# The operand tiles and the split weights of an f32r matmul stream, placed 64 bytes past a multiple of 128

## The chip, the cores and the metric

The kernel runs on one core of a Trainium2 chip. The metric is the time of one execution on the device in microseconds (us); the median of the three runs before the change is 1978.26 us (1977.85 to 1979.46).

## The reference

Two transformer-like layers on a sequence of 256 tokens, width 2048, all in float32. The first layer:

```python
h = _rmsnorm(x, pre_norm_g)
proj = h @ w_in                       # 2048 -> 1088 + 7 * 2048 columns, split into ten parts
q  = _rmsnorm(q_a)  @ w_q_b           # 512 -> 16 heads * 192
kv = _rmsnorm(c_kv) @ w_kv_b          # 512 -> 16 heads * 256
attn   = causal_attention(q, kv) * silu(z_mla);           y_mla  = attn @ w_o_mla
y_conv = (b_gate * conv3(c_gate * c_in) * silu(z_conv)) @ w_o_conv
merged = sigmoid(g_mla) * y_mla + sigmoid(g_conv) * y_conv
x = x + _rmsnorm(merged @ w_out, post_norm_g)
```

The second layer puts 16 learned rows (`meta_tokens_2`) ahead of the 256 tokens, projects 272 rows with `w_in_2` (2048 to 12368 columns), runs a top-64 attention with an indexer on 8 heads and a gated linear recurrence on 8 heads, and joins both branches:

```python
p = einsum('btnc,ncd->btnd', stack([y_a, y_b], 2), w_branch)   # two times 1024 -> 2048
merged = sum(sigmoid(gates) * p, axis=2)
h = h + merged @ w_out_2
```

What bears on this case is that nearly all of the arithmetic is matrix products of some 84 million weights (335 MB read from HBM) with 256 or 272 rows.

## The kernel before

**Units.** Activations are kept transposed: features on the 128 partitions, the 256 tokens along the free dimension. A weight matrix is worked through in units of at most 1024 elements for each partition: for most stages two k-tiles (128 input features each) of 512 output columns, that is four tiles of 128 columns; for the stage `qi` one k-tile of 1024 columns, eight tiles. `phases()` lists the stages in the order in which they run. Their matmuls are issued by `tile` in `tensor_engine`, through the helper `mm` (L1267, so that nearly every matmul carries this line).

**Split products.** Float32 precision comes from a high and a low part of both operands. For each unit, a DMA on SyncE fills one of four slots of `w_raw`; ScalarE rounds it to f32r into one of three slots of `w_hi` (`split_hi`, L1592), VectorE subtracts to get `w_lo` (`split_lo`, L1895). Activations are split in the same way into the tiles of `hb_hi`, `hb_lo` and `ob_hi`, `ob_lo`, one tile for each of 16 k-tiles. For each k-tile of each output tile, TensorE runs three matmuls: moving x_hi against the stationary w_hi, then x_lo against w_hi, then x_hi against w_lo. Each has its own load of the 128x128 stationary tile (PEld in the profile), which runs while the matmul ahead of it streams.

**Who reads which operand.** `Memory.operand` says it. `hb` is the moving operand of the stages with operand h, mg, ya and yb (the later k-tiles 8 to 15 for yb). `ob` is that of the latent projections (lat_q, lat_kv), oconv (oc), omla (zm), all second-layer projections (h2: 256 tokens from column 16 on; h2_all: all 272 columns) and the last product wout2 (mg2). In wout2 and in half of the stage kv the roles are turned: the activation tile is stationary and the weights move, in wout2 512 columns at a time.

**Places in memory.** `Memory.__init__` allocates the tensors one after another in each partition. `w_raw` begins at byte 16512, which is 129 times 128. Its 4 slots have 4096 bytes each, as have the 3 slots each of `w_hi` and `w_lo`. The four operand tensors have 16 tiles of 272 columns, 1088 bytes each, of which the 256-column stages use 1024 bytes: columns 0 to 255 in `hb` and for lat, oc and zm in `ob`, columns 16 to 271 in `ob` for h2. All seven tensors therefore begin 128 bytes past a multiple of 256.

**What sets the order.** `plan_work` fixes one order of steps for all engines ahead of time, with rings for PSUM banks, scratch tiles and slots; side work (attention, norms, recurrence) is taken in by `pump()` between units. The engines then run their own queues in that order and meet through semaphores.

Of the kernel before, what the change touches and what calls it, by code (L numbers as in the profile page):

```python
# [8 lines left out]
F32 = mybir.dt.float32  # L9
F32R = mybir.dt.float32r  # L10
I32 = mybir.dt.int32
U8 = mybir.dt.uint8
ALU = mybir.AluOpType
ACT = mybir.ActivationFunctionType
AX = mybir.AxisListType.X

P = 128
D = 2048
KT = D // P
S = 256  # L20
NMETA = 16
T = S + NMETA
# [95 lines left out]
class Stream:  # L118
# [3 lines left out]
    def __init__(self, eng, own):  # L122
        self.eng, self.own, self.count, self.seen = eng, own, 0, {}
# [67 lines left out]
class Phase:  # L191


    def __init__(self, name, weight, groups, ktiles, operand, n, period=1, pairs=False, hold=False):
        self.name, self.weight, self.groups, self.ktiles = name, weight, groups, ktiles
        self.operand, self.n, self.period, self.pairs, self.hold = operand, n, period, pairs, hold
# [827 lines left out]
PARTS1 = ((0, P), (P, 3 * P))  # L1024
HD = DN + RD
W2 = 2 * S
MAGIC = 1.5 * 2.0 ** 23
N_LVL = len(LEVELS) * P // 2
L0 = CONSTS["late"][0]
# [5 lines left out]
class Memory:  # L1035


    def __init__(self, nc, ctx, a):
        def sb(name, shape, dt=F32):
            return ctx.enter_context(nc.sbuf_tensor(name, shape, dt))  # L1040

        self.raw = sb("w_raw", [P, N_RAW, UNIT])
        self.whi = sb("w_hi", [P, N_SPLIT, UNIT], F32R)
        self.wlo = sb("w_lo", [P, N_SPLIT, UNIT], F32R)
        self.hb_hi, self.hb_lo = (sb(n, [P, KT, T], F32R)[:, :, 0:S] for n in ("hb_hi", "hb_lo"))
        self.ob_hi, self.ob_lo = sb("ob_hi", [P, KT, T], F32R), sb("ob_lo", [P, KT, T], F32R)
        self.arena = sb("arena", [P, 72 * 256])
        self.con = sb("con", [P, CONSTS["resident"][1]])
        self.cols = sb("cols", [P, P])
        self.rope1 = sb("rope1", [P, 2, S])  # L1050
        self.fac = sb("factor", [P, 3, T])
        self.small = sb("small", [P, 256])
        self.scratch = [sb(f"scratch{i}", [P, T])[:, :] for i in range(5)]
        self.heads = [sb(f"head_factor{i}", [P, T])[:, :] for i in range(3)]
        self.acc_a, self.acc_b = sb("acc_a", [P, S])[:, :], sb("acc_b", [P, S])[:, :]
        psum = [ctx.enter_context(nc.psum_tensor(f"bank{i}", [P, 512], F32))[:, :] for i in range(8)]
        self.proj, self.side = psum[:5], psum[5:]
        self.stats = [sb(f"stats{i}", [P, 8])[:, :] for i in range(6)]
        self.prob = [sb(f"prob{i}", [P, 416])[:, :] for i in range(2)]
        self.prob_t = [sb(f"probT{i}", [P, 384])[:, :] for i in range(2)]  # L1060
        self.small2, small3 = sb("small2", [P, 64]), sb("small3", [P, 2 * HI])
        self.q_factor = sb("q_factor", [P, 2 * HA])
        self.best = sb("best", [P, 16])

        r = self.region
        self.Q1, self.QR, self.K1 = r(0, 16, H1, S), r(16, 8, H1 // 2, S), r(24, 16, H1, S)
        self.V1, self.G1 = r(40, 16, 2, D), r(56, 16, KT, S)
        self.LAT = self.V1[:, 0, :].rearrange("p (k n) -> p k n", k=8)
        self.OUT1, self.GM, self.XR = r(40, 16, KT, S), self.K1, r(24, 16, KT, S)
        self.x_in, self.x_meta, self.xT = r(0, 16, 2, D), r(16, 8, D), self.G1  # L1070
        self.rows_in, self.pos_i = r(24, 1, P), r(25, 1, S)[0:1, :].bitcast(I32)
        self.u_t, self.gate_t = r(56, 4, 4, S), r(60, 4, 4, S)
        self.kr1 = r(68, 1, S)
        self.KR2, self.KI2 = r(64, 2, 2, S), r(48, 2.25, 2, T)
        self.pos_f, self.metaT = self.small[0:1, 0:S], self.small[:, :]
        self.metaf = self.metaT.rearrange("p (k n) -> p k n", k=KT)
        s2 = self.small2
        self.lb, self.oml, self.lbx, self.mx = s2[:, 0:8], s2[:, 8:16], s2[:, 16:32], s2[:, 32:40]
        self.acc_m, self.rkv_col, self.q_gain = s2[:, 40:56], s2[:, 56:58], s2[:, 58:59]
        self.wiT = small3[:, :]  # L1080
        self.R, self.RR, self.RQ = self.fac[:, 0, 0:S], self.fac[:, 1, 0:S], self.fac[:, 2, 0:S]
        self.F2 = self.fac[:, 1, :]
        self.F2M = self.F2[:, NMETA:T]

        self.QI, self.KI = r(0, 8, 8, S), r(8, 2, T)
        self.KA, self.QA, self.VA = r(9.25, 4.25, KVA, T), r(13.5, 8, HA, S), r(21.5, 6, 3, 512)
        self.FB, self.IB, self.QB = r(27.5, 8.5, HB, T), r(36, 12, 3, 1024), r(48, 8, HB, S)
        self.GA, self.GB = r(56, 16, KT, S), r(29, 16, KT, S)
        self.late = r(58, 6, CONSTS["late"][1] - L0)
        self.bias2, self.score2 = r(65, 2, 416), r(67, 2, 416)  # L1090
        self.lvl, self.lvl_in = self.small[:, 0:N_LVL // 4].bitcast(U8), r(69, 2, N_LVL)
        self.prob_m = [self.rope1[:, i, :] for i in range(2)]
        self.Cb, self.Rb, self.kL, self.qL = r(0, 2, W2), r(2, 2, W2), r(4, 2, W2), r(6, 2, W2)
        self.A, self.kK, self.kd, self.St, self.kM = r(8, 2, W2), r(10, 2, W2), r(12, 1, S), r(21.5, 2, W2), r(23.5, 4, 1024)
        self.xT2, self.OT = r(29, 16, KT, S), r(0, 16, 2, D)

        self.x_dram = nc.dram_tensor("x_kept", [P, KT * S], F32, kind="Internal").ap()
        self.x1_dram = nc.dram_tensor("x1_kept", [P, KT * S], F32, kind="Internal").ap()
        self.weights = {n: a[n] for n in ("w_in", "w_q_b", "w_kv_b", "w_o_conv", "w_o_mla", "w_out")}
        self.weights |= {"w_in_2": a["w_in_2"][0], "w_branch_a": a["w_branch_2"][0, 0],  # L1100
                         "w_branch_b": a["w_branch_2"][0, 1], "w_out_2": a["w_out_2"][0]}
# [20 lines left out]
    def operand(self, name, k):  # L1122

        if name in ("h", "mg", "ya"):
            return self.hb_hi[:, k, :], self.hb_lo[:, k, :]
        if name == "yb":
            return self.hb_hi[:, k + 8, :], self.hb_lo[:, k + 8, :]
        if name == "h2":
            return self.ob_hi[:, k, NMETA:T], self.ob_lo[:, k, NMETA:T]
        if name == "h2_all":  # L1130
            return self.ob_hi[:, k, :], self.ob_lo[:, k, :]
        k += 4 * (name == "lat_kv")
        return self.ob_hi[:, k, 0:S], self.ob_lo[:, k, 0:S]

    def out_of(self, u, m, bank):

# [439 lines left out]
def scalar_engine(nc, m, a, plan, S_):  # L1576

    sc, done, act = Stream(nc.scalar, S_("act_own")), plan.done, nc.scalar.activation
# [57 lines left out]
    def latent_split(s):  # L1636
        which, t = s.args
        k = 4 * (which == "kv") + t
        sc.wait_ge(*s.of["x"])
        sc.wait_ge(*done["cols"])  # L1640
        act(m.ob_hi[:, k, 0:S], m.LAT[:, k, :], ACT.Copy, scale=m.col(which + "a", t)).then_inc(S_("op_hi"), 1)

    def v(s):
        g, blk = s.args
# [40 lines left out]
    def conv_split(s):  # L1685
        j, t = s.args
        k = 4 * j + t
        sc.wait_ge(*s.of["y"])
        sc.wait_ge(*done["lat_used"])
        act(m.ob_hi[:, k, 0:S], m.u_t[:, t, :], ACT.Copy).then_inc(S_("op_hi"), 1)  # L1690

    def gate(s):
        name, k = s.args
# [159 lines left out]
    def x1_turn(s):  # L1853
# [6 lines left out]

    does = dict(first_loads=first_loads, split_hi=split_hi, constants=constants, x_tile=x_tile, x_keep=x_keep, sine=sine,
                bounds_exp=bounds_exp, meta_turn=meta_turn, latent=latent, latent_split=latent_split, v=v,
                scores1=scores1, turn1=turn1, mix1=mix1, cgate=cgate, zconv=zconv, conv_split=conv_split, gate=gate,
                z_sig=z_sig, z_split=z_split, merge_split=merge_split, out1=out1, meta_scale=meta_scale,
# [17 lines left out]
def vector_engine(nc, m, plan, S_):  # L1882
# [3 lines left out]
    tt, ts, stt = v.tensor_tensor, v.tensor_scalar, v.scalar_tensor_tensor  # L1886
# [59 lines left out]
    def turns(s):  # L1946
# [5 lines left out]
        ve.wait_ge(*t)  # L1952
        ve.step(ts(k_, k_, MAGIC, MAGIC, ALU.add, ALU.subtract))

# [52 lines left out]
    def latent_split(s):  # L2007
        which, t = s.args
        k = 4 * (which == "kv") + t
        ve.wait_ge(*s["op_hi"])  # L2010
        stt(m.ob_lo[:, k, 0:S], m.LAT[:, k, :], m.col(which + "a", t), m.ob_hi[:, k, 0:S].bitcast(F32),
            ALU.mult, ALU.subtract).then_inc(S_("op_lo"), 1)

    def kr(s):
# [83 lines left out]
    def conv_split(s):  # L2098
        j, t = s.args
        k = 4 * j + t  # L2100
        ve.wait_ge(*s["op_hi"])
        tt(m.ob_lo[:, k, 0:S], m.u_t[:, t, :], m.ob_hi[:, k, 0:S].bitcast(F32), ALU.subtract).then_inc(S_("op_lo"), 1)

    def gate(s):
        name, k = s.args
# [471 lines left out]
```

## Time and profile before

| | us |
|---|---|
| median of 3 runs | 1978.26 |
| the profiled execution | 1978.3 |
| its span, first to last instruction | 1977.0 |
| PE busy | 1952.0 (15786 matmuls) |
| PEld busy | 1920.3 |
| DVE busy | 1176.7 |
| ACT busy | 879.2 |
| POOL busy | 317.0 |
| DMA, mean rate | 174 GB/s |

Busy times are sums of the time in which an engine had an instruction under way. Matmuls are pipelined: one that the profile gives as 0.28 us long is followed by the next 0.12 us later, so for a stream of them the distance between starts is the measure, not the length. The distance is read either from two rows of the timeline and the number of matmuls between them, or from a window laid from the first start of a stage to the first start of the next.

### The profile page before, as it was taken

The numbers are of one execution on the slowest core, as the hardware profiler recorded it, in microseconds if no ns is written. First come the engines' busy times: TensorE is split into PE (matmuls) and PEld (weight loads), VectorE is DVE, ScalarE is ACT, GpSimd is POOL, SyncE is SP. The second block draws the span as 40 slices with busy tenths as digits, with TensorE's granted clock in tenths as the row PEclk, the third lists the DMA queues.
The fourth block names the chain that finished last, engine by engine and source line by source line (L and its number), as shares of the span: only waits on it lengthen the run. The fifth ranks groups of instructions, "written<-read, shape, count | busy, mean of one in ns | idle before, by whom it ended". The sixth has DMA issues, their size and how long they took to land.

```text
span 1977.0 us, 37092 instructions
## 1 busy us (share of the span) xinstructions
PE 1952.0 (99%) x15786; PEld 1920.3 (97%) x15786; DVE 1176.7 (60%) x1707; ACT 879.2 (44%) x1264; POOL 317.0 (16%) x320
## 2 busy tenths in 40 slices
PE   7999999999999999999999999999999999999999
PEld 7999999999999999999999999999999999999987
DVE  6765665655554445654554574676457687564644
ACT  5444454444444434544444543445443333444443
POOL 3110010202010001300121253040011132110200
PEclk9999999999999999999999999999999999999999
DMA  7565445555555555555565564443555444565564
GB/s 248 155 192 177 153 148 159 161 180 182 184 185 187 183 189 183 182 183 189 183 226 185 165 213 139 139 140 117 158 177 155 139 131 138 180 193 184 183 232 159
DMA packets 175647, 343.79 MB, mean 174 GB/s; under 512 B 10478, under 2 KB 19050, under 8 KB 174954
## 3 DMA queue, kind: packets, MB, share of 16 engines
q1 hardware_dynamic: 174106, 337.16, 53.7%
q10 hardware_dynamic: 1376, 4.26, 0.6%
q8 instruction: 124, 2.03, 0.4%
q14 instruction: 41, 0.34, 0.0%
HBM read 335.09 MB, written 6.29 MB: 173 GB/s over the span
## 4 chain that ended last, share of the span: by engine, by line
PE 92%; DVE 2%; issue 1%; ACT 1%; POOL 0%; POOLq 0%; ACTq 0%; DVEq 0%
PE bank L1267 91%; DVE w_lo L1895 1%; ACT w_hi L1592 0%; DVE arena L2166 0%; DVE hb_lo L2127 0%; DVE ob_lo L2171 0%; DVE arena L2160 0%; DVE scratch L1997 0%; POOL scratch L2487 0%; PE bank L1474 0%; PE bank L1563 0%; PE bank L1414 0%; PE bank L1413 0%; PE bank L1412 0%; PE bank L1564 0%
## 5 line engine op out<-in xcount | busy, mean ns | idle before, releaser
L1895 DVE TENSOR_TENSOR w_lo<-w_raw,w_hi 128x1024 fp32r<-128x1024 f32 (+2 forms) x644 | 786.0, 1225 | 502.0 <-ACT w_hi L1592 500.0
L1592 ACT ACTIVATE w_hi<-w_raw 128x1024 fp32r<-128x1024 f32 (+2 forms) x644 | 662.4, 1031 | 910.8 <-PE bank L1267 905.8
L1267 PE MATMUL bank<-hb_hi,w_hi 128*128 128x256 f32 x2448 | 697.9, 285 | 3.2 <-DVE w_lo L1895 3.2
L1267 PE MATMUL bank<-hb_hi,w_lo 128*128 128x256 f32 x2448 | 690.0, 282 | 0.0
L1267 PE MATMUL bank<-hb_lo,w_hi 128*128 128x256 f32 x2448 | 688.2, 281 | 0.0
L1267 PE MATMUL bank<-ob_hi,w_hi 128*128 128x256 f32 (+1 forms) x2224 | 645.7, 290 | 5.1 <-DVE ob_lo L2171 2.6
L1267 PE MATMUL bank<-ob_hi,w_lo 128*128 128x256 f32 (+1 forms) x2224 | 627.4, 282 | 0.0
L1267 PE MATMUL bank<-ob_lo,w_hi 128*128 128x256 f32 (+1 forms) x2224 | 626.3, 282 | 0.0
L1267 PEld LDWEIGHTS bank<-hb_hi,w_hi 128*128 128x128 f32 x2448 | 464.7, 190 | 5.3 <-DVE w_lo L1895 3.9
L1267 PEld LDWEIGHTS bank<-hb_hi,w_lo 128*128 128x128 f32 x2448 | 462.5, 189 | 0.0
L1267 PEld LDWEIGHTS bank<-hb_lo,w_hi 128*128 128x128 f32 x2448 | 461.7, 189 | 0.4
L1267 PEld LDWEIGHTS bank<-ob_hi,w_hi 128*128 128x128 f32 x2224 | 420.4, 189 | 8.2 <-DVE w_lo L1895 3.6
L1267 PEld LDWEIGHTS bank<-ob_lo,w_hi 128*128 128x128 f32 x2224 | 420.2, 189 | 1.5
L1267 PEld LDWEIGHTS bank<-ob_hi,w_lo 128*128 128x128 f32 x2224 | 419.5, 189 | 0.0
L1267 PE MATMUL bank<-arena 128*128 128x64 f32 (+4 forms) x618 | 101.6, 302 | 2.5 <-ACT arena L1812 1.5
L1267 PEld LDWEIGHTS bank<-arena 128*128 128x128 f32 x618 | 80.8, 191 | 4.8 <-ACT arena L1812 2.3
L2497 POOL TENSOR_TENSOR arena<-scratch,arena 128x256 f32<-128x256 f32 x32 | 38.4, 1225 | 272.8 <-DVE scratch L1997 272.8
L1997 DVE TENSOR_TENSOR scratch<-bank,factor 128x256 f32<-128x256 f32 (+1 forms) x132 | 52.7, 420 | 39.4 <-PE bank L1267 38.6
L1267 PE MATMUL bank<-w_hi,ob_hi 128*128 128x512 f32 (+1 forms) x192 | 69.0, 359 | 0.0
L1267 PE MATMUL bank<-w_lo,ob_hi 128*128 128x512 f32 (+1 forms) x192 | 68.5, 357 | 0.0
L1267 PE MATMUL bank<-w_hi,ob_lo 128*128 128x512 f32 (+1 forms) x192 | 68.4, 356 | 0.0
L2470 POOL TENSOR_TENSOR arena<-arena,factor 128x256 f32<-128x256 f32 x16 | 19.2, 1226 | 272.8 <-DVE arena L1997 272.8
(237 smaller groups left out, 1209.8 us busy)
## 6 DMA issues: line engine op xcount, KB each, us to landing
w_raw<-in_w_in SPq DMA_DIRECT2D x436, 512.0 KB, 3.5
w_raw<-in_w_out SPq DMA_DIRECT2D x64, 512.0 KB, 4.2
w_raw<-in_w_o_conv SPq DMA_DIRECT2D x32, 512.0 KB, 3.7
w_raw<-in_w_o_mla SPq DMA_DIRECT2D x32, 512.0 KB, 3.7
w_raw<-in_w_branch SPq DMA_DIRECT2D x32, 512.0 KB, 3.5
w_raw<-in_w_kv_b SPq DMA_DIRECT2D x16, 512.0 KB, 3.7
w_raw<-in_w_q_b SPq DMA_DIRECT2D x16, 384.0 KB, 3.3
arena<-x_kept SPq DMA_DIRECT2D x2, 2048.0 KB, 8.9
```

The source lines that it names most:

```text
L1267: return nc.tensor.matmul(dst, lhsT, rhs, start=start, stop=stop, skip_group_check=True)
L1592: act(dst, src, ACT.Copy).then_inc(S_("w_hi"), 1)
L1895: tt(low, src, high.bitcast(F32), ALU.subtract).then_inc(S_("w_lo"), 1)
L1997: tt(dst, m.proj[s.of["pb"]][:, 0:dst.shape[1]], factor, ALU.mult).then_inc(S_("evac"), 1)
L2470: tt(m.u_t[:, t, :], m.u_t[:, t, :], m.R, ALU.mult).then_inc(S_("conv_b"), 1)
L2497: tt(y, m.scratch[s.of["scratch"].slot][:, 0:S], y, ALU.add).then_inc(S_("merged"), 1)
```

## The change

The diff adds an unused tensor of 16 floats (64 bytes) ahead of `w_hi`, so that the split weights and all that follows move by 64 bytes. `hb_hi` and `hb_lo` become the two halves of one tensor whose tiles follow each other every 1024 bytes, with 16 floats of padding behind it. The tiles of `ob_hi` and `ob_lo` become 288 columns (1152 bytes) apart, and the stages that use 256 of them all take columns 16 to 271; lat, oc and zm used columns 0 to 255 before. No instruction is added or removed, and none changes its size. `w_raw` stays where it is; `arena` and the tensors behind it move by 128 bytes as a whole.

```diff
@@ -1024,6 +1024,7 @@
 W2 = 2 * S
+ODD = 16
 MAGIC = 1.5 * 2.0 ** 23
@@ -1040,10 +1041,12 @@
         self.raw = sb("w_raw", [P, N_RAW, UNIT])
+        sb("odd", [P, ODD])
         self.whi = sb("w_hi", [P, N_SPLIT, UNIT], F32R)
         self.wlo = sb("w_lo", [P, N_SPLIT, UNIT], F32R)
-        self.hb_hi, self.hb_lo = (sb(n, [P, KT, T], F32R)[:, :, 0:S] for n in ("hb_hi", "hb_lo"))
-        self.ob_hi, self.ob_lo = sb("ob_hi", [P, KT, T], F32R), sb("ob_lo", [P, KT, T], F32R)
+        hb = sb("hb", [P, 2 * KT * S + ODD], F32R)[:, 0:2 * KT * S].rearrange("p (k n) -> p k n", k=2 * KT)
+        self.hb_hi, self.hb_lo = hb[:, 0:KT, :], hb[:, KT:2 * KT, :]
+        self.ob_hi, self.ob_lo = (sb(n, [P, KT, T + ODD], F32R)[:, :, 0:T] for n in ("ob_hi", "ob_lo"))
         self.arena = sb("arena", [P, 72 * 256])
@@ -1130,7 +1133,7 @@
         k += 4 * (name == "lat_kv")
-        return self.ob_hi[:, k, 0:S], self.ob_lo[:, k, 0:S]
+        return self.ob_hi[:, k, NMETA:T], self.ob_lo[:, k, NMETA:T]
@@ -1638,7 +1641,7 @@
-        act(m.ob_hi[:, k, 0:S], m.LAT[:, k, :], ACT.Copy, scale=m.col(which + "a", t)).then_inc(S_("op_hi"), 1)
+        act(m.ob_hi[:, k, NMETA:T], m.LAT[:, k, :], ACT.Copy, scale=m.col(which + "a", t)).then_inc(S_("op_hi"), 1)
...
```

The three places left out (L1690, L2011, L2102) make the same replacement of `0:S` by `NMETA:T` where ScalarE and VectorE write these tiles.

## Rows read from the trace of the kernel before

**Rows 1.** The page: busy time by engine, granted clock, and the chain that ended last.
```profile
PE 1952.0 (99%) x15786; PEld 1920.3 (97%) x15786; DVE 1176.7 (60%) x1707; ACT 879.2 (44%) x1264; POOL 317.0 (16%) x320
...
PEclk9999999999999999999999999999999999999999
...
PE 92%; DVE 2%; issue 1%; ACT 1%; POOL 0%; POOLq 0%; ACTq 0%; DVEq 0%
```
**Rows 2.** Groups of PE by form: count | busy us, mean ns | idle before, releaser.
```profile
L1267 PE MATMUL bank<-hb_hi,w_hi 128*128 128x256 f32 x2448 | 697.9, 285 | 3.2 <-DVE w_lo L1895 3.2
...
L1267 PE MATMUL bank<-ob_hi,w_hi 128*128 128x256 f32 x1824 | 524.2, 287 | 5.1 <-DVE ob_lo L2171 2.6 <-DVE w_lo L1895 2.4
...
L1267 PE MATMUL bank<-ob_hi,w_hi 128*128 128x272 f32 x400 | 121.5, 304 | 0.0
...
L1267 PE MATMUL bank<-w_hi,ob_hi 128*128 128x512 f32 x128 | 51.0, 398 | 0.0
```
**Rows 3.** Windows of oconv, gmla, part of gb, bb: length, PE busy (x), clock.
```profile
653.45:744.66 91.21, 91.21 (x771) 1.00 0.56 185
836.25:927.64 91.39, 91.39 (x770) 1.00 0.58 185
1757.02:1824.72 67.70, 67.70 (x579) 1.00 0.63 194
1836.00:1881.39 45.39, 45.39 (x386) 1.00 0.55 183
```
**Rows 4.** Timeline of stage qi: first matmul of nine units; and one later matmul.
```profile
1122.66 0.28 PE L1267 MATMUL bank<-ob_hi,w_hi 128*128 128x256 f32 x1
...
1125.51 0.28 PE L1267 MATMUL bank<-ob_hi,w_hi 128*128 128x256 f32 x1
...
1128.23 0.28 PE L1267 MATMUL bank<-ob_hi,w_hi 128*128 128x256 f32 x1
...
1131.09 0.28 PE L1267 MATMUL bank<-ob_hi,w_hi 128*128 128x256 f32 x1
...
1133.92 0.28 PE L1267 MATMUL bank<-ob_hi,w_hi 128*128 128x256 f32 x1
...
1136.76 0.28 PE L1267 MATMUL bank<-ob_hi,w_hi 128*128 128x256 f32 x1
...
1139.59 0.28 PE L1267 MATMUL bank<-ob_hi,w_hi 128*128 128x256 f32 x1
...
1140.54 0.28 PE L1267 MATMUL bank<-ob_hi,w_lo 128*128 128x256 f32 x1
...
1142.46 0.28 PE L1267 MATMUL bank<-ob_hi,w_hi 128*128 128x256 f32 x1
...
1145.29 0.28 PE L1267 MATMUL bank<-ob_hi,w_hi 128*128 128x256 f32 x1
```
**Rows 5.** Timeline of wout2: first two matmuls of two units, one after the other.
```profile
1929.39 0.39 PE L1267 MATMUL bank<-w_hi,ob_hi 128*128 128x512 f32 x1
1929.62 0.40 PE L1267 MATMUL bank<-w_hi,ob_lo 128*128 128x512 f32 x1
...
1932.17 0.40 PE L1267 MATMUL bank<-w_hi,ob_hi 128*128 128x512 f32 x1
1932.41 0.39 PE L1267 MATMUL bank<-w_hi,ob_lo 128*128 128x512 f32 x1
```
**Rows 6.** Timeline of oconv: three matmuls of k-tile 0 against the second weight tile.
```profile
654.16 0.29 PE L1267 MATMUL bank<-ob_hi,w_hi 128*128 128x256 f32 x1
...
654.53 0.28 PE L1267 MATMUL bank<-ob_hi,w_hi 128*128 128x256 f32 x1
```

More of the change, by code:

```diff
@@ L1689, in conv_split @@
         sc.wait_ge(*done["lat_used"])
-        act(m.ob_hi[:, k, 0:S], m.u_t[:, t, :], ACT.Copy).then_inc(S_("op_hi"), 1)
+        act(m.ob_hi[:, k, NMETA:T], m.u_t[:, t, :], ACT.Copy).then_inc(S_("op_hi"), 1)
     def gate(s):
@@ L2010, in latent_split @@
         ve.wait_ge(*s["op_hi"])
-        stt(m.ob_lo[:, k, 0:S], m.LAT[:, k, :], m.col(which + "a", t), m.ob_hi[:, k, 0:S].bitcast(F32),
+        stt(m.ob_lo[:, k, NMETA:T], m.LAT[:, k, :], m.col(which + "a", t), m.ob_hi[:, k, NMETA:T].bitcast(F32),
             ALU.mult, ALU.subtract).then_inc(S_("op_lo"), 1)
@@ L2101, in conv_split @@
         ve.wait_ge(*s["op_hi"])
-        tt(m.ob_lo[:, k, 0:S], m.u_t[:, t, :], m.ob_hi[:, k, 0:S].bitcast(F32), ALU.subtract).then_inc(S_("op_lo"), 1)
+        tt(m.ob_lo[:, k, NMETA:T], m.u_t[:, t, :], m.ob_hi[:, k, NMETA:T].bitcast(F32), ALU.subtract).then_inc(S_("op_lo"), 1)
     def gate(s):
```

## The prediction

> **What bounds the kernel.** I read the page first: TensorE is busy for 99% of the span, at full granted clock in all 40 slices, and the chain that ended last is PE for 92% [rows 1]. VectorE at 60%, ScalarE at 44% and the DMA have room. The groups by form say what TensorE does: 2448 triples of 256-column matmuls that move `hb`, 1824 that move `ob`, 400 of 272 columns, 128 that move 512 weight columns, with 3.2 and 5.1 us of waiting ahead of the two largest groups [rows 2]. So the time is a count of matmuls times the distance between their starts, and nothing that other engines do matters unless it makes TensorE wait.
>
> The windows give that distance. In oconv 768 matmuls take 91.21 us, 118.8 ns each; gmla, which moves `hb`, 91.39 us, 119.0 ns; 576 of gb 67.70 us, 117.5 ns; the 384 of bb 45.39 us, 118.2 ns [rows 3]. (The counts in these rows have two or three more, which began before the window.) 256 columns at 2.4 GHz are 106.7 ns, so some 11 ns of each step are something else, and the step differs between stages whose instructions are the same. Nothing waits in these windows: busy equals length.
>
> **Where the step depends on place.** Stage qi is a natural experiment, because there one activation tile moves for a whole unit of 24 matmuls. What counts for me is the distance of the moving tile from the stationary tile, modulo 256 bytes. The weights all lie 128 past a multiple of 256, and tile k of h2 lies 128 + 64 + 1088k, so the distance is 64(k+1) modulo 256. The first rows of nine units [rows 4] give, divided by 24:
> - k = 2, distance 192: 2.72 us, 113.3 ns. k = 6, the same distance: 2.83 us, 117.9 ns.
> - k = 4 and 8, distance 64: 2.83 us each, 117.9 ns.
> - k = 1 and 5, distance 128: 2.85 and 2.84 us, 118.8 and 118.3 ns.
> - k = 3 and 7, distance 0: 2.86 and 2.87 us, 119.2 and 119.6 ns; once settled, the last 16 steps of k = 7 take 1142.46 - 1140.54 = 1.92 us, 120.0 ns.
>
> Two things follow: place is worth up to 6.7 ns a step, and a place can hold more than one rhythm (113.3 and 117.9 at 192).
>
> Is it the distance, or the moving tile's own place? In wout2 the weights move and their place modulo 256 never changes; the stationary activation tile does. Two units that follow each other begin with a step of 0.23 us and one of 0.24 us [rows 5], and in the timeline this pattern alternates with the pairs of stationary tiles (k = 0, 1 against k = 2, 3). The place of the stationary tile therefore counts too, which is what two reads that get in each other's way would do. I take the distance as what decides.
>
> **The change, part by part.**
> - `hb`: before, its tiles stood at distances 0, 64, 128, 192 in turn. After, the weights lie 192 past a multiple of 256, and so does every tile of `hb`, which is 1024 bytes long: distance 0, for all 2448 triples. Both were moved by the same 64 bytes. The bounds are 119.2 ns, the unit k = 3 [rows 4], and the worst triple at distance 0, the one in oconv, 654.53 - 654.16 = 0.37 us or 123 ns a step [rows 6]; I take the settled 120.0, since here nothing leaves distance 0. Of the 7344 matmuls, 6576 (h, mg) stood at 118.8 by oconv, which walks through the same four distances: +1.2 x 6576 = +7.9 us. The 768 of ya and yb stood at bb's 118.2: +1.8 x 768 = +1.4 us.
> - `ob`, 256 columns: a tile is 1152 bytes, so used from column 16 the tiles lie 64 and 192 past a multiple of 256 in turn: distances 128 and 0. Mean of 118.5 and 120.0: 119.3 ns (bounds 118.3 and 120.0). The 2016 matmuls of oc, zm, lat_q and lat_kv stood at 118.8: +0.5 x 2016 = +1.0 us. The 3456 of h2 stood at gb's 117.5: +1.8 x 3456 = +6.2 us. This is half the cost though these tiles hardly move: h2 already lay 64 past in half its tiles, and it loses the 192 that gives 113.3.
> - `ob`, 272 columns (h2_all, 1200 matmuls): now 0 and 128, distances 64 and 192, the good ones. At 256 columns the mean of these (117.9, and 113.3 or 117.9) is 116.8, that of all four about 117.9: -1.1 x 1200 = -1.3 us.
> - wout2 and the turned half of kv (576 matmuls): distances 128 and 0 instead of four. Rows 5 show steps of 0.23 and 0.24 us at different places; at 1 ns either way this is ±0.6 us, taken as 0.
> - Writes of the split tiles by ScalarE and VectorE keep their sizes; w_raw's DMA is unchanged. If they grew by a few per cent, the 40% of VectorE's span that is free would hide it. The 64 bytes of `odd` cost no instruction. `arena`, `con` and the rest move together, so side matmuls keep their distances: 0.
>
> Sum: 7.9 + 1.4 + 1.0 + 6.2 - 1.3 = +15.2 us. The profiled execution took 1978.3 us (span 1977.0), as the median does (1978.26). Where TensorE waits for a split, a slower step is absorbed; with 3.2 + 5.1 us of such idle [rows 2] I take off 0.5. That gives 1993.0 us, 0.75% slower. The likeliest case's own range is 1984 (119.2 for `hb`, 118.3 for `ob`) to 2001.
>
> The Trainium skill speaks against any of this: "TensorE: Matmul & The Clock Gate", Part 2, step 1, says that TensorE has two independent read ports, so that loading the next tile's weights takes no bandwidth from the running matmul, and its formula for the back-to-back gap, N/2.4 + 2.5, would be 109 ns at 256 columns wherever the operands lie. The trace disagrees, with 113.3 to 120.0 ns in one stage [rows 4].
>
> **The rivals.**
> - *Only the moving tile's own place counts* (0.19). Then rows 4 read by absolute place: 192 past a multiple of 256 (k = 4, 8) is 117.9, 64 past (k = 2, 6) 113.3 or 117.9, mean 115.6; 0 and 128 past are the slow ones, and the change moves all 256-column tiles off them. `hb` all at 117.9: -0.9 x 6576 - 0.3 x 768 = -6.1 us; `ob` at the mean of 117.9 and 115.6, 116.8: -2.0 x 2016 - 0.7 x 3456 = -6.5 us; h2_all goes to the slow places, +1.3. Sum -11.3: 1967 us, faster. For it: every odd multiple of 64 is below every even one in rows 4. Against it: wout2, where the stationary place shows. It wins if that influence is small for 256 columns.
> - *Distance 0, held throughout, settles in a quicker rhythm* (0.08). Distance 192 has two, 4.6 ns apart. At 118 ns `hb` would save 0.8 x 6576 + 0.2 x 768 = 5.4 us and `ob` cost some 4: 1976 us, within or a little past no change. Against it: units k = 3 and 7 come from different neighbours and both go to 120.
> - *It does nothing* (0.06): the step follows the order of instructions and not places, and the patterns of rows 4 are an accident of it. 1978.3 us. The reads being independent, as the page above has it, would give this.
> - *A worse rhythm at distance 0* (0.03): 123 ns as in rows 6 for all of `hb`: +4.5 x 7344 = +33 us, 2018 us with `ob`. Against it: such triples stand only right after a change of distance.
>
> **How the numbers follow.** The likeliest case has 0.64. A measurement of this kernel tells 0.2%, about 4 us, from no change. Slower by more than that: 0.62 of the likeliest, the worse rhythm's 0.03 and 0.01 of the quicker rhythm's case, 0.66. Within: 0.02 + 0.06 + 0.04 = 0.12. Faster: 0.19 + 0.03 = 0.22. The range runs from 1966 to 2001: it leaves out half of the first rival, the worse rhythm and the tail of the likeliest.
>
> **What would show it.** If I am right, gmla's window is 768 x 120.0 = 92.2 us instead of 91.39 and bb's 46.1 instead of 45.39; units of qi take 2.84 to 2.88 us and none 2.72; the 272-column groups have lower means. If the moving place alone counts, gmla's window is 90.5 us. If `hb` stages keep steps of different lengths although their distance never changes, the picture of two reads that meet modulo 256 bytes is wrong as such. Idle time of TensorE should stay as it is in every case.

## The result, and the profile after

The changed kernel takes 1987.82 us, the median of four runs (1987.09 to 1988.31), against 1978.18 before: a ratio of 1.0047 [1.003, 1.0065]. It is slower, by 9.6 us where the forecast had 14.7. The profiled execution has a span of 1985.8 us, 8.8 more than before.

The page after, busy time by engine, granted clock and the chain that ended last:

```profile
PE 1961.1 (99%) x15786; PEld 1930.5 (97%) x15786; DVE 1177.1 (59%) x1707; ACT 880.0 (44%) x1264; POOL 316.7 (16%) x320
...
PEclk9999999999999999999999999999999999999999
...
PE 92%; DVE 2%; ACT 1%; issue 1%; POOL 0%; POOLq 0%; ACTq 0%
```

Against [rows 1], PE is busy for 9.1 us more with the same 15786 instructions and the same granted clock (0.998 on the mean of both spans); the load of the stationary tiles (PEld) for 10.2 us more, and the other engines stand within 1 us. So the time came from inside the stream of matmuls, and not from a wait.

The groups of PE by form after (count | busy us, mean ns | idle before, releaser):

```profile
L1270 PE MATMUL bank<-hb,w_hi 128*128 128x256 f32 x4896 | 890.1, 284 | 3.0 <-DVE w_lo L1898 2.9
...
L1270 PE MATMUL bank<-ob_hi,w_hi 128*128 128x256 f32 x1824 | 522.1, 286 | 4.9 <-DVE ob_lo L2174 2.6 <-DVE w_lo L1898 2.3
...
L1270 PE MATMUL bank<-ob_hi,w_hi 128*128 128x272 f32 x400 | 121.1, 303 | 0.0
```

`hb` is one tensor now, so its first two products share a name and a row (4896 = 2 x 2448). Idle time ahead of the two largest groups is 3.0 and 4.9 us, where [rows 2] had 3.2 and 5.1. The mean durations hardly tell anything (286 for 287 ns on `ob_hi` though its stages changed in both directions): a pipelined matmul's length is not its step.

The steps are in the windows of oconv, gmla, omla, gb and bb, each from its first start to the next stage's first start (length, PE busy (x), clock, ...):

```profile
657.11:747.57 90.46, 90.46 (x770) 1.00 0.59 187
839.85:932.07 92.22, 92.22 (x771) 1.00 0.62 183
932.07:1023.37 91.30, 91.30 (x770) 1.00 0.57 185
1752.73:1844.20 91.47, 91.47 (x771) 1.00 0.62 184
1844.20:1890.28 46.08, 46.08 (x387) 1.00 0.57 181
```

bb has 384 matmuls in 46.08 us: 120.0 ns. gmla's 92.22 us are 120.1 ns for 768, and 759 of its steps in the trace are 120 ns to the nanosecond. Both are what the prediction wrote down, 46.1 and 92.2. But oconv went down, from 91.21 [rows 3] to 90.46 us, which is 117.8 ns a step, while omla, with the same instructions on the same operand addresses, takes 91.30 us, 118.9 ns.

The timeline of stage qi after, the first matmul of six units, k = 1 to 6:

```profile
1127.97 0.28 PE L1270 MATMUL bank<-ob_hi,w_hi 128*128 128x256 f32 x1
...
1130.84 0.28 PE L1270 MATMUL bank<-ob_hi,w_hi 128*128 128x256 f32 x1
...
1133.69 0.28 PE L1270 MATMUL bank<-ob_hi,w_hi 128*128 128x256 f32 x1
...
1136.56 0.28 PE L1270 MATMUL bank<-ob_hi,w_hi 128*128 128x256 f32 x1
...
1139.42 0.28 PE L1270 MATMUL bank<-ob_hi,w_hi 128*128 128x256 f32 x1
...
1142.29 0.28 PE L1270 MATMUL bank<-ob_hi,w_hi 128*128 128x256 f32 x1
```

The first five units take 2.87, 2.85, 2.87, 2.86, 2.87 us, and the next three, in the trace, between 2.85 and 2.88. Odd k stand at distance 0 now and even k at 128. The quick unit of 2.72 us in [rows 4] is gone, as predicted. Step by step (starts to the nanosecond), distance 0 settles at 120, 120, 120, ..., and distance 128 repeats 119, 115, 118, 122, 120: the same five steps that units at distance 128 showed before the change, when they lay at other places. These distances differ by whole multiples of 256 bytes from unit to unit (the tiles lie 1152 bytes apart), and all eight units at distance 0 settle at 120 ns; so it is the distance modulo 256 that counts.

One thing is not as foreseen. In gconv, whose moving tiles all stand at distance 0, 558 of the 768 steps are not 120 ns: from the 79th step on the trace shows 124, 118, 117, 121, 120, over and over, and a part of zmla does the same. The mean of these five is 120.0 too, so no time comes of it (gconv takes 92.26 us, gmla 92.22), but one distance does not mean one step.

### The profile page after: what moved, and what is told of

Its sections match the earlier page's. It is cut to its first block, busy times and chain, and to the rows that moved or that the text cites. A ratio compares the mean times of both kernels' runs of the same rounds, so it can differ in the third digit from the quotient of the medians.

```text
span 1985.8 us, 37092 instructions
## 1 busy us (share of the span) xinstructions
PE 1961.1 (99%) x15786; PEld 1930.5 (97%) x15786; DVE 1177.1 (59%) x1707; ACT 880.0 (44%) x1264; POOL 316.7 (16%) x320
## 4 chain that ended last, share of the span: by engine, by line
PE 92%; DVE 2%; ACT 1%; issue 1%; POOL 0%; POOLq 0%; ACTq 0%
PE bank L1270 91%; DVE w_lo L1898 1%; DVE arena L2169 1%; ACT w_hi L1595 0%; DVE ob_lo L2174 0%; DVE arena L2163 0%; POOL scratch L2490 0%; PE bank L1477 0%; PE bank L1415 0%; PE bank L1567 0%; PE bank L1417 0%; PE bank L1566 0%; PE bank L1416 0%; PE bank L1479 0%; ACT ob_hi L1750 0%
## 5 line engine op out<-in xcount | busy, mean ns | idle before, releaser
L1270 PE MATMUL bank<-hb,w_hi 128*128 128x256 f32 x4896 | 890.1, 284 | 3.0 <-DVE w_lo L1898 2.9
L1270 PEld LDWEIGHTS bank<-hb,w_hi 128*128 128x128 f32 x4896 | 764.1, 192 | 4.9 <-DVE w_lo L1898 3.6
L1270 PE MATMUL bank<-hb,w_lo 128*128 128x256 f32 x2448 | 693.1, 283 | 0.0
L1270 PEld LDWEIGHTS bank<-hb,w_lo 128*128 128x128 f32 x2448 | 469.1, 192 | 0.0
L2490 POOL TENSOR_TENSOR scratch<-scratch,head_factor 128x256 f32<-128x256 f32 x16 | 12.6, 786 | 242.6 <-ACT head_factor L1708 242.6
L2000 DVE TENSOR_TENSOR arena<-bank,factor 128x256 f32<-128x256 f32 (+1 forms) x86 | 34.6, 421 | 24.5 <-PE bank L1270 24.3
```

Source lines behind the costliest of these rows:

```text
L1270: return nc.tensor.matmul(dst, lhsT, rhs, start=start, stop=stop, skip_group_check=True)
L2000: tt(dst, m.proj[s.of["pb"]][:, 0:dst.shape[1]], factor, ALU.mult).then_inc(S_("evac"), 1)
L2490: tt(z, z, ring[s.of["head"].slot][:, 0:S], ALU.mult).then_inc(S_("silu"), 1)
```

## The experiments

Three kernels (`e1_sweep`, `e4_rhythms`, `e8_pairs`) are streams of matmuls alone and leave out the whole computation but for rounding one block of `w_in` to f32r; the others compute all of it. In a stream, "step" is the distance between starts, from the trace.

**1. A stream at sixteen distances.** The body of the loop is the kernel's triple, on a pool of f32r data:

```python
w = w0 // 4 + 128 * (m % 4)
x = (w0 + ds[m % len(ds)]) // 4
wh, wl = pool[:, w:w + 128], pool[:, WL + w:WL + w + 128]
xh, xl = pool[:, XH + x:XH + x + n], pool[:, XL + x:XL + x + n]
nc.tensor.matmul(dst, wh, xh, start=m % 2 == 0, stop=False, skip_group_check=True)
nc.tensor.matmul(dst, wh, xl, start=False, stop=False, skip_group_check=True)
inst = nc.tensor.matmul(dst, wl, xh, start=False, stop=m % 2 == 1, skip_group_check=True)
```

Here `w0` is the place of the weights and `ds` the distance, or the distances in turn, in bytes.

> Leaves the whole computation out but for a stream of f32r matmuls on one place of memory; only the distance between starts is of use. Blocks of 96 matmuls of 256 columns in the kernel's order (x_hi by w_hi, x_lo by w_hi, x_hi by w_lo, four weight tiles in turn), the moving tile d = 0, 16, ... 240 bytes past a multiple of 1024 while the weights stay at one; then blocks with weights and tile both moved by 64 and by 32 bytes, short blocks that change d in every order, blocks of 512 and of 128 columns, and blocks whose tile alternates. Theory 1 (the distance of the moving from the stationary tile modulo 256 decides): d = 0 settles at 120.0 ns, 64 at 117.8, 128 at 118.6, 192 at 113.3 or 117.8, and the blocks moved by 64 or 32 as a whole repeat these to 0.3 ns. Theory 2 (each tile's own place counts): the blocks moved by 64 differ from the unmoved ones of the same distance by 1 ns or more. Theory 3 (the rhythm is set by the order of instructions, not by place): all blocks of 256 columns lie within 1 ns. At 128 columns the weight load should be the bound, with the same step of about 113 ns as the quickest rhythm at 256; at 512 I expect 225 to 235 ns.

Windows of `e1_sweep`: 96 matmuls of 256 columns each at distance 64, 112, 128, 192; then 48 each at distances 0, 64, 128 and 192 with weights and moving tile both 64 bytes on; then 48 of 512 columns at distance 0 and 192; then 96 of 128 columns at distance 0 and 192:

```profile
70.20:81.51 11.31, 11.31 (x99) 1.00 0.01 1
...
104.55:115.43 10.88, 10.88 (x99) 1.00 0.01 2
115.43:126.81 11.38, 11.38 (x99) 1.00 0.01 1
160.92:171.81 10.89, 10.89 (x99) 1.00 0.01 2
205.86:211.60 5.74, 5.74 (x50) 1.00 0.00 0
211.60:217.26 5.66, 5.66 (x51) 1.00 0.01 3
217.26:222.96 5.70, 5.70 (x51) 1.00 0.00 0
222.96:228.43 5.47, 5.47 (x50) 1.00 0.00 0
...
299.17:310.07 10.90, 10.90 (x50) 1.00 0.00 0
332.23:343.43 11.20, 11.20 (x49) 1.00 0.01 1
343.43:354.10 10.67, 10.67 (x97) 1.00 0.00 0
...
375.54:386.26 10.72, 10.72 (x98) 1.00 0.01 2
```

The mean of the last 24 steps of each block at 256 columns, worked out from the starts (the last of them is the step into the next block):

| distance | 0 | 16 | 32 | 48 | 64 | 80 | 96 | 112 |
|---|---|---|---|---|---|---|---|---|
| ns | 120.0 | 118.7 | 116.7 | 118.3 | 117.8 | 120.0 | 120.0 | 113.3 |

| distance | 128 | 144 | 160 | 176 | 192 | 208 | 224 | 240 |
|---|---|---|---|---|---|---|---|---|
| ns | 118.7 | 118.5 | 117.3 | 119.3 | 113.3 | 119.2 | 118.3 | 117.4 |

There is no other work here, next to no DMA (a share of 0.01) and no side matmul. What is left to differ is the place, and what ran before, which the short blocks below show. With both operands moved together by 64 bytes the steps settle at 120.0, 117.8, 118.8 and 113.3 again, and by 32 bytes the same: the distance decides, and not where either operand lies. Two more readings. At 512 columns the order is turned round: 226.7 ns at distance 0 (10.90 us / 48 is 227), 228.9 at 64, 232.3 at 128, 233.3 at 192. At 128 columns all four distances settle at a mean of 111.7 ns, though 128 columns are only 53 ns at 2.4 GHz: there something that does not depend on distance sets the step. The load of the stationary tile, which has the same size in all cases, is my guess; no run tests it.

Short blocks of 24 in the same run enter one distance from another. Distance 192 entered from 0 or 128 goes to 113.3, entered from 64 it keeps the 117.8 that 64 had; 128 settles either in the five steps (118.8 on the mean) or in 118, 120, 122 (120.0). Which rhythm a distance takes depends on what ran before it.

**2. The tiles moved, the weights not.** The unused tensor goes behind the weights, so that `hb` stands at distance 64 and the 256-column tiles of `ob` at 192 and 64 in turn:

```diff
         self.raw = sb("w_raw", [P, N_RAW, UNIT])
-        sb("odd", [P, ODD])
         self.whi = sb("w_hi", [P, N_SPLIT, UNIT], F32R)
         self.wlo = sb("w_lo", [P, N_SPLIT, UNIT], F32R)
+        sb("odd", [P, ODD])
```

> The changed kernel with the 64 bytes of odd behind w_lo instead of ahead of w_hi: the operand tiles lie exactly where the change puts them, the weights where they were. Distances: 64 for all of hb, 192 and 64 in turn for ob at 256 columns, 128 and 0 for h2_all. Theory 1 (distance decides): hb at 117.8, 1.0 below before, ob between 115.6 and 117.8: 10 to 14 us faster than before, 1964 to 1968 us, ratio 0.993 to 0.995. Theory 2 (the tiles' own place decides): as the changed kernel, 1988 us, ratio 1.005. Theory 3 (neither): 1978 us.

It takes 1965.89 us, a ratio of 0.9935 [0.9922, 0.9949]. The windows of oconv, gmla, gb and bb:

```profile
646.18:735.78 89.60, 89.60 (x770) 1.00 0.60 189
826.56:917.30 90.74, 90.72 (x771) 1.00 0.63 186
1733.51:1823.50 89.99, 89.88 (x771) 1.00 0.63 187
1823.49:1868.72 45.23, 45.23 (x386) 1.00 0.58 186
```

bb's 45.23 us are 117.8 ns, the step of distance 64 in the stream. Every moving tile lies exactly where it lies in the changed kernel, since the 64 bytes stand ahead of `hb` in both; only the weights differ, and 22 us lie between the two kernels. With the 64 bytes behind the weights instead of ahead of them, the change would have made the kernel faster. oconv settles at 116.7 ns. At distance 64, cin0 ran at 113.3 and cgate0 at 115.0 before the stages went to 117.8, and zmla ran at 116.7, so 64 has more than one rhythm as well.

**3. `hb` alone at distance 0**, on multiples of 128 bytes, with nothing moved by 64. This is the `hb` term of the sum by itself, at other places than the change has it:

```diff
-        self.hb_hi, self.hb_lo = (sb(n, [P, KT, T], F32R)[:, :, 0:S] for n in ("hb_hi", "hb_lo"))
+        hb = sb("hb", [P, 2 * KT * S], F32R)[:, :].rearrange("p (k n) -> p k n", k=2 * KT)
+        self.hb_hi, self.hb_lo = hb[:, 0:KT, :], hb[:, KT:2 * KT, :]
```

> The kernel before with one edit: the tiles of hb lie every 1024 bytes, so all at a multiple of 128 and at distance 0 from the weights, which are not moved; ob as before. Nothing lies 64 past a multiple of 128 in hb. Theory 1 (distance decides): the hb stages run at 120.0 ns a matmul as in the changed kernel, +9 us, ratio 1.0045 to 1.005. Theory 2 (it is lying 64 past a multiple of 128 that made the changed kernel slower): not slower than before, 1976 to 1979 us.

1986.28 us, 1.0041 [1.0028, 1.0054]. Windows of oconv, gmla, gb, bb:

```profile
658.57:749.78 91.21, 91.21 (x771) 1.00 0.59 185
841.99:934.24 92.25, 92.25 (x770) 1.00 0.62 183
1753.51:1844.10 90.59, 90.55 (x771) 1.00 0.63 186
1844.10:1890.17 46.07, 46.07 (x386) 1.00 0.57 183
```

The stages of `hb` are those of the changed kernel (92.22 and 46.08 there), those of `ob` are those of before ([rows 3]; oconv 91.21). So 7.8 us (1986.28 - 1978.44, the median of the kernel before that was taken beside it) are the price of `hb` at distance 0, and all the rest of the change is worth about 1.8 us (9.6 - 7.8).

**4. How firm each rhythm is.** A stream in which one of five different sets of float32 side matmuls runs ahead of each block of 36, at 23 distances:

```python
for c in ((128, 128), (256,), (1, 1, 1), (128, 128, 128), (64, 64, 64, 64))[j]:
    nc.tensor.matmul(dst[:, 0:c], raw[:, 0:128], raw[:, 512:512 + c], start=True, stop=True, skip_group_check=True)
...
```

Twelve triples as in experiment 1 follow each set.

> As e1_sweep leaves the whole computation out; a stream of f32r matmuls of 256 columns with fixed weights' place. For each distance 0, 16, ... 240 and for 4, 8, 12, 104, 108, 116, 120 bytes, five blocks of 36 matmuls, each entered after a different few float32 matmuls of 128, 256, 1 or 64 columns, as side work in the kernel does. Theory A (each distance has a small set of steady rhythms and the disturbance picks one): all five blocks of a distance end in one of at most two or three means; 0 always ends at 120.0, 192 and 64 at 113.3 or 117.8. Theory B (the rhythm belongs to the distance alone): the five blocks of a distance end alike, and those of e1_sweep's place are repeated: 112 and 192 at 113.3, 32 at 116.7, 64 at 117.8.

The last 23 steps of two blocks at distance 112 and two at 192 (after the third and the fourth set):

```profile
207.88:210.49 2.61, 2.61 (x26) 1.00 0.00 0
212.68:215.29 2.61, 2.61 (x26) 1.00 0.00 0
...
329.67:332.38 2.71, 2.71 (x25) 1.00 0.00 0
334.55:337.16 2.61, 2.61 (x25) 1.00 0.00 0
```

2.61 us / 23 is 113.5 ns, 2.71 / 23 is 117.8. Of the five blocks at 192 one settles at 113.3 and four at 117.8; at 112 all five settle at 113.3; at 0 four stand at 120.0 and one comes to it within its last 12 steps (119.1); at 64 three stand at 117.8 and two at 113.3. Off the multiples of 16 there are worse places: 123.3 ns at 4, 116.7 or 126.7 at 8, up to 130 at 104. So a distance gives a short list of rhythms, and what ran before picks one of them. Distance 0 has only one mean, and it is a slow one; the kernel's gconv showed that two patterns of steps (120 throughout, and the five) share it.

**5. `hb` alone at distance 192**, every 1024 bytes:

```diff
-        self.hb_hi, self.hb_lo = (sb(n, [P, KT, T], F32R)[:, :, 0:S] for n in ("hb_hi", "hb_lo"))
+        hb = sb("hb", [P, 2 * KT * S + 64], F32R)[:, 48:48 + 2 * KT * S].rearrange("p (k n) -> p k n", k=2 * KT)
+        self.hb_hi, self.hb_lo = hb[:, 0:KT, :], hb[:, KT:2 * KT, :]
```

> The kernel before with the tiles of hb every 1024 bytes and all at distance 192 from the weights, which stay; ob as before. Distance theory: the hb stages run at 113.3 ns where the quick rhythm holds and at 117.8 where it does not. All quick: 6576 x 5.4 + 768 x 4.9 = 39 us faster, 1939 us; all slow: 6576 x 0.95 + 768 x 0.4 = 6.5 us faster, 1972 us. I expect stretches of both, as after side work in the first stage of e2_tiles_only (113.4 in cin0, then 117.8): 1960 to 1972 us, ratio 0.991 to 0.997. If it were only the 64 bytes past a multiple of 128 that help, all stages would go at 117.8: 1972 us.

1944.33 us (1942.78 to 1944.83), 0.9825 [0.9812, 0.9838]. Windows of oconv, gmla, gb, bb, and the first row of what PE waits for (us in total, times, longest):

```profile
633.70:724.47 90.77, 90.77 (x770) 1.00 0.59 187
813.98:901.66 87.68, 87.64 (x771) 1.00 0.66 192
1713.44:1804.03 90.59, 90.55 (x770) 1.00 0.63 186
1804.03:1847.56 43.53, 43.53 (x386) 1.00 0.60 191
```

```profile
PE bank L1268 <- DVE w_lo L1896: 7.4, 8, 3.0
```

bb's 43.53 us are 113.4 ns. That misses what was expected, 1960 to 1972 us with stretches of both rhythms: the quick one held in nearly all stages of `hb`. At 5.4 ns a step less than before (118.75 - 113.33), 7344 matmuls could give 40 us; 34 came. About 2 of the missing 6 us are new waiting: TensorE waits for `w_lo` in 8 places for 7.4 us, where it had 5.5 us in 3 before, so in places it has become quicker than the splits. The rest was not traced in full; gmla and zmla, for two, average 113.8 and 114.1 ns between waits. Against experiment 3 nothing differs but 192 bytes of place, and 42 us.

**6. `hb` alone at distance 112**, with 28 floats of padding in place of 48: a place that is on no multiple of 32 bytes, and in the table has slow neighbours on both sides.

> As e5_hb_192 with the tiles of hb at distance 112, so 16 bytes short of a multiple of 128. Distance theory: 113.3 ns as in e1_sweep's block at 112 if that rhythm is the only one there: 39 us faster, 1939 us, ratio 0.980; with a second rhythm near 118 to 120, 1965 to 1985 us. If tiles must lie 64 past a multiple of 128 to be quick, it is no faster than before, 1978 us or more.

1946.14 us, 0.9837 [0.9824, 0.9851]. Windows of gmla and bb:

```profile
813.20:901.01 87.81, 87.36 (x771) 1.00 0.66 193
1806.58:1850.13 43.55, 43.55 (x387) 1.00 0.59 190
```

These are experiment 5's to within 0.15 us. The 1.8 us between the medians do not come from `hb`: added up over its stages the two profiled executions differ by 0.3 us, in favour of 112, while qi, which moves `ob`, is 2.0 us longer here, with a granted clock of 0.5 for 10.2 us around its start instead of 6.8. No rule about multiples of 64 or 128 bytes would have found this place; the stream's table did.

**7. The weights alone**, moved by 64 bytes; three small tensors that stood elsewhere fill the gaps, so that no activation tile moves by anything but a multiple of 256:

```diff
         self.raw = sb("w_raw", [P, N_RAW, UNIT])
+        self.best = sb("best", [P, 16])
         self.whi = sb("w_hi", [P, N_SPLIT, UNIT], F32R)
         self.wlo = sb("w_lo", [P, N_SPLIT, UNIT], F32R)
+        self.q_factor, small3 = sb("q_factor", [P, 2 * HA]), sb("small3", [P, 2 * HI])
...
-        self.small2, small3 = sb("small2", [P, 64]), sb("small3", [P, 2 * HI])
-        self.q_factor = sb("q_factor", [P, 2 * HA])
-        self.best = sb("best", [P, 16])
+        self.small2 = sb("small2", [P, 64])
```

> The kernel before with w_hi and w_lo 64 bytes on and nothing else of the operands moved (small tensors fill the gaps, and arena moves by whole multiples of 256). Distances turn by one place: the pairs of k-tiles of h, mg, oc, zm and lat go from (0, 64), (128, 192) to (192, 0), (64, 128), those of h2 from (64, 128), (192, 0) to (0, 64), (128, 192). Distance theory: the two exchange their steps, oconv and gmla go from 118.8 to 117.6, gb and qb from 117.6 to 118.8: -1.2 x 8600 + 1.2 x 3456 = 6 us faster, 1972 us, ratio 0.996 to 0.998. Rival (the place of the weights matters by itself, 64 past a multiple of 128 being bad for them): all stages slower, up to the changed kernel's +9.6 us. Rival (it does not matter): 1978 us, each stage as before.

1971.14 us, 0.9965 [0.9953, 0.9978]. Windows of oconv, gmla, gb, bb:

```profile
648.77:739.01 90.24, 90.24 (x771) 1.00 0.60 187
830.02:920.58 90.56, 90.51 (x771) 1.00 0.63 187
1738.38:1829.77 91.39, 91.39 (x771) 1.00 0.62 185
1829.77:1874.88 45.11, 45.11 (x387) 1.00 0.58 186
```

Every tile of `hb` and `ob` walks through the four distances as before, but begins one place earlier (192, 0, 64, 128 where it was 0, 64, 128, 192). oconv and bb take the 117.5 ns that h2 had before and gmla 117.9, and gb takes 119.0 (768 matmuls in 91.39 us), near the 118.8 that oconv had. The stages exchanged their rhythms though no moving tile was touched. That excludes the first rival of the prediction, that only the moving tile's own place counts. It also shows that the order in which distances follow each other has its own price.

**8. Two distances in turn**: x_hi at one distance and x_lo at another, or triples that alternate, at 256 and 272 columns.

> As e1_sweep leaves the whole computation out; blocks of 48 matmuls of 256 columns and of 30 of 272, each after one float32 matmul. For each distance d of x_hi, in steps of 16 bytes: both tiles alternating between d and d + 128 as ob does in the changed kernel, and x_hi fixed at d with x_lo at d + 64 to d + 192, which is what tiles of ob every 2304 bytes for a high and a low one would give. If the distance of each matmul decides by itself, the mean of a block is that of its distances: pairs of 112 and another lie near (2 x 113.3 + 117 to 120)/3 = 115, the alternating pair 0 and 128 at 119.3, 64 and 192 at 115.6 to 117.8, as oconv in the changed kernel and in e2_tiles_only. If what came before matters, equal distances give different means in different pairs, and some pairs hold 113.3 though the x_lo's distance alone does not.

The best of 160 combinations at 256 columns settle at 115.5 ns (x_hi at 48, x_lo 80 or 128 bytes further on; 144 with 112 or 144 more; 240 with 64 more). The usual value is 117.8. Distance 112, which holds 113.3 by itself, gives 117.8 to 120.0 as soon as x_lo stands elsewhere; 192 in turn with 64 gives 116.7, and the same pair begun at 64 gives 117.8. At 272 columns the blocks settle between 122.2 and 128.9. Within what was tried, 113.3 needs one and the same distance from matmul to matmul.

One pair explains what the changed kernel did in oconv and omla, whose triples alternate between distance 128 and 0. The last 24 steps of the block that begins at 0 and of the one that begins at 128:

```profile
27.55:30.40 2.85, 2.85 (x26) 1.00 0.00 0
505.28:508.11 2.83, 2.83 (x27) 1.00 0.02 6
```

From the starts these are 118.9 and 117.8 ns. The first repeats 119, 122, 120, 113, 120, 120, which are omla's steps, the second 117, 119, 112, 119, 119, 121, which are oconv's, both with changes of 1 ns. So the two stages stand in the two rhythms of one pair of distances.

**9. All that was learned in one kernel**: weights back at 128 past a multiple of 256, `hb` and the first-layer tiles of `ob` (lat, oc, zm) every 1024 bytes at distance 192, the second layer's tiles 1152 bytes apart at distances 192 and 64.

```diff
+        sb("gap", [P, 32])
+        ob = [sb(n, [P, KT * (T + ODD)], F32R) for n in ("ob_hi", "ob_lo")]
+        self.ob_hi, self.ob_lo = (o[:, :].rearrange("p (k n) -> p k n", k=KT)[:, :, 0:T] for o in ob)
+        self.o1_hi, self.o1_lo = (o[:, ODD:ODD + KT * S].rearrange("p (k n) -> p k n", k=KT) for o in ob)
+        hb = sb("hb", [P, ODD + 2 * KT * S], F32R)[:, ODD:].rearrange("p (k n) -> p k n", k=2 * KT)
...
-        return self.ob_hi[:, k, 0:S], self.ob_lo[:, k, 0:S]
+        return self.o1_hi[:, k, :], self.o1_lo[:, k, :]
```

> A version made from the findings. Weights where they were; all tiles of hb every 1024 bytes at distance 192, as in e5_hb_192; in the first layer the tiles of ob (lat, oc, zm) are used every 1024 bytes too, all at distance 192; in the second layer, where 272 columns are needed, they lie every 1152 bytes, at 192 and 64 in turn as in e2_tiles_only. Distance theory: hb as in e5_hb_192, 34 us faster than before; the 2016 matmuls of lat, oc and zm at 113.4 instead of 118.8, 10.8 us; h2 at 116.7 to 117.5 instead of 117.6, 0 to 3 us. Sum 45 to 48 us: 1931 to 1934 us, ratio 0.976 to 0.978. Rival (as the quick rhythm nears the pace of the split weights, TensorE waits for w_lo more often): the waits of TensorE grow by the amount that the steps shrink in some stages, 1940 us or more.

1939.8 us (1935.78 to 1947.54), 0.9816 [0.9796, 0.9836]: the quickest median of all, but less of a gain than expected and with a wider spread. Windows of oconv, gmla, gb, bb, and the first row of PE's waits:

```profile
632.40:719.44 87.04, 87.04 (x771) 1.00 0.62 195
808.43:896.18 87.75, 87.33 (x770) 1.00 0.65 193
1706.55:1797.31 90.76, 90.65 (x771) 1.00 0.63 186
1797.31:1842.53 45.22, 45.22 (x386) 1.00 0.58 185
```

```profile
PE bank L1274 <- DVE w_lo L1902: 8.9, 11, 3.2
```

oconv got its 113.3 ns (87.04 / 768). bb, at the same distance 192 as in experiment 5, took the other rhythm: 45.22 us against 43.53, 117.8 ns against 113.4. gb gained nothing: its steps without a wait are 117.7 ns in the trace, where [rows 3] have 117.5. This is experiment 4 inside the real kernel: a place with two rhythms pays only when the quick one is caught, and with 192 that is left to what runs ahead of it. The rival of the expectation, more waiting, has a smaller share: the waits for `w_lo` are 1.5 us more than in experiment 5, and bb alone is 1.7 us longer. The interval overlaps experiment 5's, so that kernel, two lines from the original and steadier, is the one I would keep, or experiment 6's, whose distance settled in the quick rhythm in all five blocks of experiment 4.

## Why the prediction was right, and where its size was off

**The mechanism.** That the time follows the distance between moving and stationary tile modulo 256 bytes held wherever it was tried: moved together, nothing changes (experiment 1); weights moved alone, stages change (7); tiles moved by different amounts, the `hb` stages follow the distance (2, 3, 5, 6). But the distance gives a list of rhythms and not a step. The prediction had named a sign against its own picture, "if `hb` stages keep steps of different lengths although their distance never changes", and gconv shows it: 124, 118, 117, 121, 120 at distance 0 throughout. The mean of 120.0 that the forecast used held all the same; the picture of two reads that meet modulo 256 bytes, each step by itself, is too simple. That it is reads at all is argued from the effect and not shown. What waits for what, and why 112 and 192 are the good ones, stays open: the profile shows when matmuls start, and nothing inside the step. The Trainium skill, in "TensorE: Matmul & The Clock Gate", Part 2, step 1, has two independent read ports, and its section "Back-to-back issue gap" gives N/2.4 + 2.5 ns for a matmul by itself, an estimate of 109 ns at 256 columns, which the prediction took for a stream with loads. The runs show 113.3 to 120.0 ns by place at multiples of 16 bytes, and even the best place stays 4 ns above that estimate.

**The terms**, each against the change in length of its stages between the two profiled executions (first start of a stage to that of the next, added up):

| term | forecast | measured |
|---|---|---|
| `hb`, h and mg | +7.9 | +6.1 |
| `hb`, ya and yb | +1.4 | +1.2 |
| `ob`, oc, zm, lat (with the turned half of kv) | +1.0 | -0.8 |
| `ob`, h2 | +6.2 | +2.7 |
| `ob`, 272 columns | -1.3 | -0.4 |
| wout2 | 0 | -0.1 |
| absorbed by waits | -0.5 | within the rows above |
| sum | +14.7 | +8.7 |

The spans differ by 8.8 us; the first matmul of the first stage starts 0.05 us later. So `hb` came out near its forecast (7.3 of 9.3 us) and gave most of the time, and `ob` far below (1.5 of 5.9 us): the sign and the cause were right, and the size of the `ob` terms was not.

- *h, mg, ya, yb: right.* 120.0 ns were forecast and 120.0 came (bb 46.08 us, gmla 92.22). Of the 2.0 us that are missing 0.9 are in the first stage, qa, and most of that (some 0.7 us) has nothing to do with place: the granted clock of 0.5 with which the kernel starts ended 4.9 us into qa before and 3.2 us after the change, so that 15 steps instead of 22 ran at about 213 ns. The rest is spread over many stages, most of it in those with side matmuls, whose steps are 119.8 to 119.9 on the mean. Experiment 3 has the term by itself, 7.8 us in the medians.
- *oc and zm: the step that failed in sign.* "Mean of 118.5 and 120.0: 119.3 ns" took the step of a walk through two distances to be the mean of their own steps. oconv settled at 117.8 and omla at 118.9, below 119.3 and one of them even below the 118.8 of before. Two distances in turn have rhythms of their own: experiment 8 has both of these for the pair 0 and 128, 117.8 and 118.9, step by step.
- *h2: the term that made most of the difference.* The same wrong mean, which is worth about 1.6 us here: 119.3 was forecast, and in gb, zb and qb the steps without a wait are 118.8 to 118.9, 1.3 ns more than before and not 1.8. In qa2, ga and za, with side matmuls between, they rose by 0.4 to 0.7 ns only. And in qi, where the step rose by 1.5 ns, TensorE waits for splits: it lost 0.4 us less in steps that a wait lengthens, 0.1 us less at the granted clock of 0.5, and the stage's length changed by 0.02 us. The prediction had taken off 0.5 us for waits in the whole kernel; qi alone used that up.
- *272 columns: right in sign, a third of the size.* The steps went from 125.5 to 125.2 ns. Taking the difference of 256-column steps for those of 272 columns was the guess there; experiment 1 shows at 512 columns that the order of distances can even turn round with the length.
- *Waits as before, no other engine: right* (3.0 and 4.9 us against 3.2 and 5.1, other engines within 1 us).
- *The range:* with the bounds that the prediction names for its low end, 119.2 ns for `hb` and 118.3 ns for `ob`, its own terms add up to 1982 us and not 1984; and the full clock in all 40 slices is a reading of rounded digits, since 6.8 us at the start of qi have a granted clock of 0.5 in both kernels. Neither changes the outcome.

**The rivals.** That only the moving tile's place counts fell to experiments 2 and 7: in 2 every moving tile lies where the changed kernel has it, and the time is 22 us less. A quicker rhythm at distance 0 did not come in the changed kernel, nor in experiment 3, nor in the blocks at distance 0 of experiments 1 and 4. A worse rhythm of 123 ns at distance 0 did not come either: steps of 124 ns recur in gconv and zmla, every fifth, but in a rhythm whose mean is 120.0. "Nothing" is excluded by the interval of the ratio and by bb's 0.69 us.

## What to carry to other kernels

When TensorE is busy for 99% at full clock, and the count of matmuls can't be cut, divide the length of a quiet window by its matmuls: steps that differ between stages with equal instructions are a reason to look at the places of the operands. Alignment of one operand alone did not tell the quick places here; measure the step of the kernel's own triple against the distance between moving and stationary tile in one run of a stream, then give all tiles of a stage one distance that is quick after every disturbance tried, and keep it from matmul to matmul. A mean of two places' steps doesn't forecast a walk through both. Part of what a quicker stream wins goes to the waits behind it: of 40 us at distance 192 34 came, and 2 of the missing 6 were new waits.

## What the runs showed of the hardware that was not expected

- Place alone moves the step of a 256-column f32r matmul between 113.3 and 120.0 ns at multiples of 16 bytes, and to 130 ns off them (experiments 1, 4). For the whole kernel this was 42 us, between 1944.33 and 1986.28, with 192 bytes of difference in one allocation.
- The step has memory. The same instructions on the same operand addresses ran at 117.8 ns in oconv and 118.9 in omla of the changed kernel, and those of bb at one distance, 192, at 113.4 or 117.8 (experiments 5, 9).
- What is best at 256 columns (192: 113.3 ns) is worst of four at 512 (233.3 against 226.7 at distance 0), and at 128 columns the four settled means are equal (111.7).
- At a granted clock of 0.5 (1.2 GHz) place showed nothing: in the first unit of qi the steps are 213.3 ns on the mean at distance 64 (before) and at distance 128 (after), which is 256 columns at 1.2 GHz with nothing added.
- TensorE can lose time over places in memory with all other engines idle (experiment 1). The Trainium skill, "SBUF — State Buffer", section "Who interferes with whom", says that TensorE never waits on anyone there. As far as other engines go, nothing here contradicts it; but within TensorE the places of its two operands relative to each other do matter, by up to 6.7 ns a step at 256 columns.
